# The first modulation in column quarters beside the first GLU units, and four smaller reorderings, in a one-core encoder step

## The reference

```python
sh1, sc1, g1, sh2, sc2, g2 = split(silu(c) @ w_ada + b_ada, 6)   # c: 9 vectors, w_ada 2048 x 12288
h = rmsnorm(x, norm1_g) * (1 + sc1) + sh1
za, zg, q, k, v = split(h @ w_in, [1024, 2048, 3072, 4096])      # w_in 2048 x 5120
u = za * sigmoid(zg)                                             # GLU
y_conv = silu(layernorm(causal_dwconv(u, w_dw) + b_dw))          # width 31
o = band_attention(q, k, v)
x = x + g1 * (concat(y_conv, o) @ w_out)
h2 = rmsnorm(x, norm2_g) * (1 + sc2) + sh2
# PEER: per row and head the best 16 of 128 x 128 experts
s = (h2 @ w_pq) . sub_keys ; top 16 of each half, top 16 of their sums
out = sum_e softmax(.)_e * gelu(h2 . u_experts[e]) * v_experts[e]
x = x + g2 * out ;  y = rmsnorm(x, final_g)
```

## Time and profile before

| | us |
|---|---|
| median of 3 timed runs | 3962.62 |
| lowest, highest | 3953.63, 3974.74 |
| profiled execution, span from first to last instruction | 3945.3 |
| TensorE busy (matmul) | 3630.9, 92% |
| VectorE busy | 2664.1, 68% |
| ScalarE busy | 446.6, 11% |
| POOL busy | 1088.6, 28% |

### The profile page before, as it was taken

One profiled execution on the slowest core, in us unless ns is written; L12 is line 12 of the kernel. 1 busy time (PEld: TensorE's weight loads), 2 busy tenths in 40 slices (PEclk: granted clock), 3 DMA queues, 4 the chain that ended last, 5 costly groups with the idle time before them and its releaser, 6 DMA issues.

```text
span 3945.3 us, 34389 instructions
## 1 busy us (share of the span) xinstructions
PE 3630.9 (92%) x12423; PEld 1928.8 (49%) x12423; DVE 2664.1 (68%) x4415; ACT 446.6 (11%) x975; POOL 1088.6 (28%) x865
## 2 busy tenths in 40 slices
PE   4899998997996799789989999999989899999997
PEld 1566544466552574356833444444455344444443
DVE  1258852148888885878976766677688765555666
ACT  2100004110000350011700000000043000000000
POOL 1000001106434543444153222222234422222331
PEclk8999999998998779899999999999999999999998
DMA  9878763459999998999699999999978999999997
GB/s 364 278 233 265 246 214 124 150 195 393 410 413 417 370 379 326 396 386 398 228 415 421 421 414 418 421 418 416 421 285 337 420 420 396 421 422 421 422 418 311
DMA packets 348738, 1402.89 MB, mean 356 GB/s; under 512 B 25601, under 2 KB 150489, under 8 KB 207606
## 3 DMA queue, kind: packets, MB, share of 16 engines
q0 software_dynamic: 117056, 832.57, 52.4%
q1 hardware_dynamic: 230512, 563.29, 38.1%
q10 hardware_dynamic: 1008, 4.98, 0.3%
HBM read 1375.24 MB, written 31.55 MB: 357 GB/s over the span
## 4 chain that ended last, share of the span: by engine, by line
DMA 48%; PE 27%; issue 14%; DVE 8%; POOL 3%; ACT 0%; SPq 0%; DVEq 0%; POOLq 0%; ACTq 0%
DMA R<-in_u_experts,MS 34%; DMA R<-in_v_experts,MS 10%; PE bank L868 8%; PE bank L896 7%; PE bank L1083 4%; DMA R<-in_w_ada 3%; POOL R L749 3%; DVE R L2242 2%; PE bank L808 1%; DVE R L2127 1%; DVE R L2034 1%; PE bank L785 1%; PE bank L1090 1%; DMA R<-h_scratch 1%; PE bank L1145 1%
## 5 line engine op out<-in xcount | busy, mean ns | idle before, releaser
L749 POOL DMA_INDIRECT R<-in_u_experts,MS x640 | 899.9, 1406 | 1639.2 <-DVE MS L2127 1354.6
L2127 DVE CUSTOM_DVE_ANT_0 R<-R 128x2048 f32<-128x2048 f32 x374 | 857.2, 2292 | 412.0 <-DMA R<-in_u_experts,MS 390.7
L1290 PE MATMUL bank<-R,RB 128*128 128x512 f32 x2304 | 1019.4, 600 | 46.9 <-DMA R<-in_v_experts 46.7
L1290 PE MATMUL bank<-RB 128*128 128x512 f32 x1792 | 778.2, 592 | 0.0
L1290 PEld LDWEIGHTS bank<-R,RB 128*128 128x128 f32 x2304 | 440.7, 192 | 615.5 <-issue 552.9
L2127 DVE CUSTOM_DVE_ANT_0 R<-R,RB 128x2048 f32<-128x2048 f32 x266 | 608.5, 2288 | 107.1 <-DMA R<-in_u_experts,MS 105.7
L1290 PEld LDWEIGHTS bank<-RB 128*128 128x128 f32 x1792 | 340.5, 190 | 428.6 <-issue 428.6
L2242 DVE SCALAR_TENSOR_TENSOR R<-R,MS 128x2048 f32<-128x2048 f32 x128 | 301.4, 2355 | 197.3 <-DMA R<-in_v_experts,MS 196.9
L868 PE MATMUL bank<-RB,R 128*128 128x256 f32 (+1 forms) x1536 | 400.4, 422 | 27.6 <-DMA R<-in_w_pq 24.4
L868 PEld LDWEIGHTS bank<-RB,R 128*128 128x128 f32 x1536 | 294.5, 193 | 126.4 <-DMA R<-in_w_pq 25.0
L1083 PE MATMUL bank<-RB,R 128*128 128x384 f32 x1024 | 333.3, 486 | 1.4 <-ACT RB L1450 0.7
(11 more groups left out here) (353 smaller groups left out, 2214.4 us busy)
## 6 DMA issues: line engine op xcount, KB each, us to landing
R<-in_v_experts SPq DMA_DIRECT2D x144, 1024.0 KB, 9.1
RB<-in_v_experts SPq DMA_DIRECT2D x112, 1024.0 KB, 9.3
R<-in_w_ada SPq DMA_DIRECT2D x48, 2048.0 KB, 13.2
R<-in_w_in SPq DMA_DIRECT2D x20, 2048.0 KB, 18.0
R<-in_w_in SPq DMA_DIRECT2D x24, 1024.0 KB, 28.4
R<-in_w_out SPq DMA_DIRECT2D x8, 2048.0 KB, 8.2
R<-in_w_pq SPq DMA_DIRECT2D x8, 2048.0 KB, 10.1
R<-in_w_out SPq DMA_DIRECT2D x16, 1024.0 KB, 15.9
```

The costliest lines, as they stand in the source:

```text
L749: pool.indirect_dma_start(dst, None, table, bass.IndirectOffsetOnAxis(ap=expert[T_ % 2][:, c:c + 1], axis=0)).then_inc(signal, 16)
L1290: x = pe.matmul(PB[4 * h + q][:, :], W[:, i, h * P:(h + 1) * P], vring[slot][:, q * PW:(q + 1) * PW], start=(i == 0), stop=(i == NKEY - 1))
L2127: V.tensor_tensor_reduce(u, u, x, 1.0, 0.0, ALU.mult, ALU.add, dots[t % 2][:, h * TOPK + s:h * TOPK + s + 1]).then_inc(dots_done, 1)
```

## The change

1. SP loads x first, then the first modulation in 32 pieces of 1 MB: column quarter q of the scale and of the shift, four k-tiles each. POOL's setup moves ahead of its small inputs, the conv cache moves up. ScalarE squares three tiles of x and VectorE two. The first two `w_in` blocks are loaded behind the first four pieces.
2. A piece is 4 matmuls, each k-tile in its own group of PE columns (stationary operand `cT32`, 32 columns wide). ScalarE copies the bank, and `turn_mods(q)` sums the four groups with a 0/1 column matrix, adds the bias and turns in one go. The first four units (two value, two gate) run k-tile by k-tile beside the pieces of the next quarter.
3. The 12 other units have 32 halves of 512 columns and 8 k-tiles of the second modulation before them, 3, 3, 2, 3, 3, 2, ... to a unit, in slots 2 and 3.
4. The last column of the first tiles' `w_out` finishes tile 0 before tile 1 begins; row scales and transposes of tile 0 follow it.
5. Before the first dot only group 0 is chosen; the steps of group 1, and 16 of group 2, stand between the first 16 dots. In `choose` pairs of operations on 256 elements become one on 512. Some semaphores are merged.

```diff
@@ SP
-            for n in range(NM1):
-                chunk, i = (1, n) if n < 8 else (0, n - 8)
-                if n >= NRING:
-                    sp.wait_ge(mod_done, n - 3)
-                sp.dma_start(tall[:, n % 4], wv["w_ada"][:, 2 * i:2 * i + 2, chunk * D:(chunk + 1) * D]).then_inc(w_in_s[n % 4], 16)
+            for t in range(T):
+                sp.dma_start(xt[t], xp[t] if t < TP else xs).then_inc(s_x, 16)
+
+            def load_ada_piece(n):
+                q, shift, j = n // 8, n // 4 % 2, n % 4
+                if n >= 4:
+                    sp.wait_ge(mod_done, n - 3)
+                at = (0 if shift else D) + q * PW
+                sp.dma_start(ada_piece[:, j], wv["w_ada"][:, 4 * j:4 * j + 4, at:at + PW]).then_inc(s_bx[j], 16)
+
+            def load_ada_half(m):
+                c, half = divmod(m, 2)
+                sp.wait_ge(mod_done, ADA - 2 + 2 * m if m < 2 else ADA + m - 1)
+                sp.dma_start(wide[:, 2 + half], wv["w_ada"][:, 8 * half:8 * half + 8, 2 * D + c * PW:2 * D + (c + 1) * PW]
+                             ).then_inc(w_in_s[2 + half], 16)
+
+            for n in range(4):
+                load_ada_piece(n)
+            for b in range(2):
+                load("w_in", b, b * CC)
+            for n in range(4, ADA):
+                load_ada_piece(n)
+            for m in range(2):
+                load_ada_half(m)
+            for b in range(2):
+                sp.wait_ge(z_done, 2 * b + 2)
+                load("w_in", b, BW + b * CC)
+
+            m = 2
+            for u in range(12):
+                for _ in range(HALVES[u % 3]):
+                    if m < 2 * NMC:
+                        load_ada_half(m)
+                    m += 1
+                i, b, c = 1 + u // 4, u // 2 % 2, u % 2
+                if c == 1 and i < 3:
+                    sp.wait_ge(z_done, 4 + u + 1)
+                    load("w_in", b, (i + 1) * BW + b * CC)
@@ PE
+            def ada_sums(n):
+                q, shift, j = n // 8, n // 4 % 2, n % 4
+                if j == 0 and q >= 1:
+                    pe.wait_ge(s_mc, 2 * (q - 1) + shift + 1)
+                    if shift:
+                        pe.wait_ge(s_A1, q)
+                pe.wait_ge(s_bx[j], 16 * (n // 4 + 1))
+                for i in range(4):
+                    m = pe.matmul(PB[6 + shift][32 * i:32 * i + 32, :], cT32[:, 4 * j + i, :], ada_piece[:, j, i, :],
+                                  start=(j == 0), stop=(j == 3))
+                m.then_inc(mod_done, 1)
+
+            def turn_mods(q):
+                pe.wait_ge(s_mc, 2 * q + 2)
+                for shift in range(2):
+                    for i in range(4):
+                        at = (0 if shift else D) + (4 * q + i) * P
+                        out = PB[7][:, 64 * shift + 16 * i:64 * shift + 16 * i + NCND]
+                        pe.matmul(out, mrow[:, at:at + P], ident[32:32 + NCND, 32:32 + NCND],
+                                  start=True, stop=False)
+                        m = pe.matmul(out, mod_sums[shift][:, i * P:(i + 1) * P], group_sum, start=False, stop=True)
+                m.then_inc(s_modT, 1)
+
+            def modulate_half(m):
+                c, half = divmod(m, 2)
+                bank = PB[4 + (c + 2) % 4]
...
+                pe.wait_ge(w_in_s[2 + half], 16 * (c + 1))
+                for k in range(8):
+                    g = k % 4
+                    mm = pe.matmul(bank[32 * g:32 * g + NCND, :], cT[:, 8 * half + k, :], wide[:, 2 + half, k, :],
+                                   start=(half == 0 and k < 4), stop=(half == 1 and k >= 4))
+                mm.then_inc(mod_done, 1)
...
+            for n in range(4):
+                ada_sums(n)
+            turn_x(0, KT + 4)
+            turn_conv_cache()
+            for n in range(4, 8):
+                ada_sums(n)
+            pe.wait_ge(s_bada, 32)
+            turn_mods(0)
             pe.wait_ge(cc_E, 4)
+            for q in range(3):
+                n = 8 * (q + 1)
+                for i in range(4):
+                    for u in range(4):
+                        first_unit(u, 4 * q + i)
+                        if 4 * i + u in (0, 1, 3, 4, 6, 7, 9, 10):
+                            ada_sums(n)
+                            n += 1
+                        elif 4 * i + u == 12:
+                            turn_mods(q + 1)
+            for u in range(4):
+                for k in range(12, KT):
+                    first_unit(u, k)
+
+            m = 0
+            for u in range(12):
+                for _ in range(HALVES[u % 3]):
+                    modulate_half(m)
+                    m += 1
+                i, b, c = 1 + u // 4, u // 2 % 2, u % 2
+                pe.wait_ge(w_in_s[b], 16 * (i + 1))
+                pe.wait_ge(z_free, 4 + u + 1)
+                project((hTX, hTY), ring[:, b, :, c * P:(c + 1) * P], c, z_done)
@@ PE, first tiles' last column
+            weights_in(0)
+            pe.wait_ge(o_free, 7)
+            half_rows(catX, 0, 0, 0, 2)
+            weights_in(1)
+            half_rows(catX, 1, 1, 0, 2).then_inc(o_done, 1)
+            pe.wait_ge(o_free, 8)
+            half_rows(catX, 0, 0, 1, 3).then_inc(w_used, 1)
+            half_rows(catX, 1, 1, 1, 3).then_inc(o_done, 1)
+            pe.wait_ge(s_xn, T + 1)
+            for k in range(KT):
+                if k // 2 != 3:
+                    turn_xn(0, k)
...
@@ VectorE
-            for i in range(4):
-                two_blocks(8 * i)
...
+            gated(0)
+            gated(1)
+            for i, sums in enumerate((((0,), (1, 2), (3,), (4,)), ((5, 6), (7,), (8,), (9, 10)), ((11,), (12,), (13, 14), (15,)))):
+                for step in range(4):
+                    for c in sums[step]:
+                        modulated(c)
+                    if step < 2:
+                        conv(2 * i + step)
+                    else:
+                        gated(2 * i + step)
...
-                    ch.mark(TT(ea, io, taf.unsqueeze(2).to_broadcast(A16), ALU.is_equal))
-                    ch.mark(TT(eb, io, tbf.unsqueeze(2).to_broadcast(A16), ALU.is_equal))
+                    ch.mark(TT(e4, io, tab.rearrange("p (o j) -> p o j", o=2).unsqueeze(3).to_broadcast(A2), ALU.is_equal))
...
-                if g + 2 < NG and g + 2 not in (16, 17):
+                if g == 0:
+                    for q in range(s * 34 // TOPK, (s + 1) * 34 // TOPK):
+                        choose(1 + q // 18, q % 18)
+                elif g + 2 < NG and g + 2 not in (16, 17):
                     choose(g + 2, s)
...
-            for g in range(2):
-                for k in range(18):
-                    choose(g, k)
+            for k in range(18):
+                choose(0, k)
             steps(124)
```

More of the change, by code:

```diff
@@ L207, in hybrid_encoder_step @@
         dist_row = [late(256).bitcast(BF16)]
-        picks.append([late(P) for i in range(3)])
+        picks.append(late(3 * P))
         dist_row.append(late(256).bitcast(BF16))
-        first, second, weight = ([p[i] for p in picks] for i in range(3))
+        first, second, weight = ([p[:, i * P:(i + 1) * P] for p in picks] for i in range(3))
+        keys_of = [p[:, 0:2 * P].rearrange("p (o n) -> p o n", o=2) for p in picks]
         WK = 7552
@@ L371, in load @@
                 sp.dma_start(ring[:, j], wv[name][:, :, bass.ds(col, BW)]).then_inc(w_in_s[j], 16)
-            for n in range(NM1):
-                chunk, i = (1, n) if n < 8 else (0, n - 8)
-                if n >= NRING:
-                    sp.wait_ge(mod_done, n - 3)
-                sp.dma_start(tall[:, n % 4], wv["w_ada"][:, 2 * i:2 * i + 2, chunk * D:(chunk + 1) * D]).then_inc(w_in_s[n % 4], 16)
-            for j in range(2):
-                sp.wait_ge(mod_done, NM1 - 4 + j + 1)
-                load("w_in", j, j * CC)
@@ L382, in _ @@
-            for j in range(2):
-                sp.wait_ge(mod_done, NM1 - 2 + j + 1)
-                load("w_ada", 2 + j, (NM1 + j) * BW)
-            def beside(i, b, more):
-                w = i * 2 + b
-                for a in range(2, 6 if more else 4):
-                    sp.wait_ge(mod_done, w * 4 + (NM1 + a - 1))
-                    load("w_ada", 2 + a % 2, w * (4 * BW) + (NM1 + a) * BW)
-            with sp.Fori(0, 3) as i:
-                for b in range(2):
-                    beside(i, b, True)
-                    sp.wait_ge(z_done, i * 4 + (2 * b + 2))
-                    load("w_in", b, i * BW + (BW + b * CC))
@@ L883, in _, with first_unit @@
-            glu_and_modulation(0, True)
-            with pe.Fori(1, 4) as i:
-                glu_and_modulation(i, False)
-            loaded = [8, 8, 20, 20]
+            def first_unit(u, k):
+                if u == 0:
+                    pe.wait_ge(xT_act, KT + 4 + k + 1)
+                    pe.wait_ge(xT_dve, k + 1)
+                if k == 0 and u % 2 == 0:
+                    pe.wait_ge(w_in_s[u // 2], 16)
+                w = ring[:, u // 2, k, (u % 2) * P:(u % 2 + 1) * P]
```

(29 more changed lines are left out.)

307 lines of the change are left out of this document (136 added, 171 removed).

## The result

| | median us | runs |
|---|---|---|
| before | 3958.12 (3949.92 to 3974.74) | 4 |
| after | 4051.86 (4049.21 to 4067.65) | 4 |

The ratio is 1.0244, with a 95% interval of 1.0211 to 1.0277: 94 us slower, between 84 and 110. The prediction said slower, 4000, and not above 4030. The sign and the eight waits came as written; the start did not.

The account below looks back on a forecast made before the run. Transfers bound the kernel to about 125 us, TensorE until the gathers at 867, then DMA nearly everywhere. Terms +43 - 3.4 - 0 - 3 gave +37 on 3962.6, so 4000 us, range 3960 to 4030.

Parts of the forecast that it names:

- the sum of 37: Whole kernel: +43 at the end of the modulation stage, -3.4, -0 and -3 behind it, so 37 us slower.
- Part 1, the start: Start to the fourth unit's end: first unit at 62.5, four units done at 166, 30 us won.
- Part 2, the eight waits: Twelve later units: each group's third half is fetched while TensorE stands, five waits of 6.2 and three of 10, 61 us.
- Clock 12 predicted: Behind the eight waits: TensorE's clock falls, 1.5 us for each, 12 us in all.
- the ext and bias moves: 0: Moved ext and bias transfers: no cost, hidden behind TensorE or the queues.
- Part 3: Last output column of the first tiles, tile by tile: 3.4 us won, bounds 0 and 6.
- Part 4: First dots behind the first choosing: taken as 0, bounds 5 either way.
- Part 5: Merged steps of choosing: 3 us won, bounds 0 and 24.
- A microsecond lost or won before the gathers counts once at the end: All stages before 867 us: no delay there is caught up afterwards, as gather order is fixed and DMA engines are full.
- (a): Rival on the units: third halves hidden, no waits or clock loss, -36, 3927 us; chance 0.12.
- (b): Rival on start and waits: first unit at 57, waits 5.2 and 8.5, +10, 3973 us; chance 0.2.
- (c): Rival on clock and start: low clock longer behind each wait, first units late at 70, +57, 4020 us; chance 0.18.

Follow-up runs that it names:

- e3_start: Changed kernel with the two first w_in loads moved behind pieces 4 to 7 of the first modulation: 4052.65 us, ratio 1.025.
- e5_sumbias: e1_even with e3_start's load order, and b_ada added once in each bank's sums by a matmul, halving a turning's matmuls: 3964.03 us, ratio 1.0033.
- e2_fours: Changed kernel with the halves in groups of 4, 4 and 0 ahead of the units instead of 3, 3 and 2: 4072.02 us, ratio 1.0305.
- e1_even: Changed kernel with two halves ahead of each unit and one in the middle of two units of three: 3983.05 us, ratio 1.0079.
- e8_best: e9_copy with the last two halves behind the last unit, b_ada added by VectorE instead of a matmul, and the old last column: 3938.58 us, ratio 0.9969.
- e9_copy: e5_sumbias with POOL's 5 MB bias-row copy held until the second load of the first projection rows has landed: 3948.39 us, ratio 0.9985.
- b_p3: Kernel before with only the last output column of the first tiles done tile by tile: 3964.01 us, ratio 1.0033.
- b_p5: Kernel before with only the merged steps of choosing: 3948.57 us, ratio 1.0002.

## Why the prediction was wrong

By its own steps, with the result of 94 against the sum of 37. Of the 57 missing us 38 are in the start, 9 in the stage of the units, and the last 10 behind it: at the first rows the delay was 90 where 43 was forecast, and from there to the end the forecast had 6 won where 4 more were lost.

- **Part 1, the start: the step that failed.** "First unit at 62.5 ... The first four units end at 166", 30 us won. Measured: 76.9 and 204.5, so 8.6 lost (204.5 against 210.2 - 14.3 = 195.9 of before). That is 38 of the 57 missing us. The path was the right one, but its terms were mis-sized or missing:
  *First unit, 14.4 late.* The turning, put at 3.2 from a row of 16 other records, took 6.9: 3.7 (by its own price of up to 0.13 a record, 32 records are 4.1, not 3.2). x was scaled at 42.2 instead of 38, as ScalarE and VectorE waited for it until 27.5, though it was first in SP's queue: 4. Pieces 4 to 7 stood in SP's queue behind w_in: 4 (e3_start). The rest, some 3, is the sums 0 to 3, which stand ahead of x's turning in TensorE's order and held it until 45.9; I had not counted them.
  *From there to the first half, 127.6 instead of 103.6.* Three turnings: 11. A sum, priced by half of 16 records at 0.95, costs 1.20 between steps of other shapes (the steps on its two sides start 2.28 apart, in e5_sumbias 144.63 and 146.91, instead of 1.08): 24 x 0.25 = 6. The other 7 fit the lower clock behind the turnings. The same code took 121.4 and 124.1 us in e2_fours and e1_even, so some 6 us of this stretch vary from one execution to the next. e5_sumbias, with half the matmuls, took back 4 to 10 us of it, after paying 11.6 for its bias matmuls.
  That the idea of part 1 was sound, e8_best shows: 68.7 to 174.8 is 106.1 us, where the step had 103.6.
- **Part 2, the eight waits: right.** 61 us predicted, 64.5 measured, five of 6.3 to 6.6 and three of 10.2 to 12.1, ahead of the units named. Clock 12 predicted, 17.1 measured. Stage 347.9 against 339. Taking the waits away gave 65 us at the end, of 73 in the stage. The Trainium skill's figure (DMA: Bandwidth & Descriptors, Anatomy of one DMA) gave an estimate of 6.8 us for such a fetch; the traces have 7.9 and more, so rows were the better price. The section's fit is of DMAs that GpSimd issues, and these are SP's. The Trainium skill's rule of the clock falling in bursts between transfers (TensorE: Matmul & The Clock Gate, the section on HAM oscillation) agrees with all eight waits (the halves behind them took 3.3 to 3.6 instead of 1.9). The waits that the page tells of are longer than e1_even's of 1.45 us, behind which the half took 1.90.
- **A step that was not there.** POOL's copy was taken as hidden ("the ext and bias moves: 0"). The copy took no time of TensorE's own, but it met w_in at the first rows: 4.6 us of idle in after, 10.5 us at the first gather between e5_sumbias and e9_copy.
- **Part 3: wrong in sign.** 3.4 to be won, 1.8 lost at the key queries in b_p3; the price of the second half's late request (a wait of 3.8 to 4.1, in the changed kernel too) was not looked for. I had followed the load of w_pq, but not the w_out loads of the same loop.
- **Part 4, "taken as 0": holds** within its interval; the second choosing does move off the path and w_pq waits take its place. **Part 5, 3 us:** b_p5 has +1 (-7 to +9), which tells nothing of 3. The three parts together, 6.4 predicted, 6 measured: luck, since the largest of them had the wrong sign.
- **"A microsecond lost or won before the gathers counts once at the end": not a rule.** In e8_best 15.2 won at the first gather are 12 to 14 at the end, and in after some 93 lost are 94. But e1_even is 19 late at the first gather, 32 late at dot 124 and 31 (21 to 41) at the end, and b_p3 is 5.3 early there, 11 late at dot 124 and 13 (6 to 21) late at the end. How soon the dots and w_pq can follow the first gather counts too.

Of the rivals, (a) was refuted by the eight waits and (b) by the first unit at 76.9 and waits as long as forecast. (c) named the right things, a late start and more of the lower clock, but too small. The range ended at 4030, since each term of the start was bounded by its own row and no bound said that all could err the same way: they were priced from rows of other shapes, or of the same shape between other neighbours.

## What to carry over

Count slots before units: n pieces per gap with two slots means n - 2 pieces that are fetched in the open (here the third stood 6.3 us and a fourth 1.7 to 2.1 more), and moving one piece into the middle of the next unit cures it (65 us here). Price a short matmul by a row of its own shape in its own surroundings, and ask what the clock does behind it. When work is moved earlier, list also what its end releases on the other queues: here a 5 MB copy that came to lie in front of a load on the path.

## What the runs showed of the hardware

- TensorE, busy without a break, went from the full clock (102 to 104 us) to 0.50 granted (105 to 109) in 32 records with 9 columns, and the wide ones behind them began at 0.50. With half as many (e5_sumbias) the turnings beside the units stayed at the full clock.
- Issuing two loads of 2 MB held SP's queue 28.3 us while x and four pieces were in flight; issued at 46.4 (e3_start) they held it 8.2, and the issue of one such load by itself takes 0.37 (e5_sumbias, at 434.75).
- A matmul of 9 rows and 512 columns takes 0.97 us, as long as four of 128 rows on the four column groups together (0.99). Put between the first group and the other three, it made 2.93 us of 0.99 (e5_sumbias).
- One copy of 5 MB in POOL's queue stretched a 2 MB load in SP's from 8.3 to 20.0 us.
